# A Mamba-2 scan on one core: one gate SiLU, the first exponentials of sums and one mask product change their places

## The chip, the cores and the metric

One core of one Trainium2 chip runs the whole program. The metric is the device time in microseconds; lower is better. Before the change it is 2375.91 us, the median of 3 runs (2374.59 to 2376.46).

## What is computed

A two-layer decoder trunk on a sequence of 1024 tokens, width 1024, in float32. Layer 0 is a sliding-window attention beside a pooling mixer; layer 1 is a Mamba-2 mixer; a SwiGLU block follows each. The change lies in the Mamba-2 mixer alone. Its inner width of 2048 falls into 4 groups of 8 heads (512 channels), and each group runs through 8 chunks of 128 tokens. Cut to what matters:

```python
def ssd_chunked(x, dt, A, Bm, Cm):
    ...
    seg = a_cs[..., :, None] - a_cs[..., None, :]
    decay = jnp.exp(jnp.where(causal, seg, -jnp.inf))
    cb = jnp.einsum('bclgn,bcsgn->bcgls', Cc, Bc)
    y_diag = jnp.einsum('bcgls,bcghls,bcsghp->bclghp', cb, decay, xdt)
    ...
    h0 = jnp.zeros((b, G, hg, p, n), jnp.float32)
    _, prev = lax.scan(step, h0, ...)
    y_off = jnp.einsum('bclgn,bcghpn,bcghl->bclghp', Cc, prev, jnp.exp(a_cs))
    return (y_diag + y_off).reshape(b, s, h, p)

y = ssd_chunked(xs, dt, A, Bm, Cm) + xs * D[:, None]
y = y.reshape(b, s, SSD_INNER) * jax.nn.silu(z)
```

Then comes an RMS norm over each group and the output projection. The carried state before the first chunk is zero, so `exp(a_cs)` of chunk 0 multiplies zero.

## The kernel before

The five engines have a program each, in a fixed order written out by hand, and wait for one another through counting semaphores. Weights come through SyncE's queue, ScalarE makes the high part of each (`hi`, L898), GpSimd the low part (`lo`, L727, 128x1024), and TensorE multiplies in three float32 passes (L1383 to L1385).

`ssd_group` runs four times (three turns of a loop, then the last group written out). In a group, per chunk c of 8:

- TensorE turns and multiplies the chunk's operands for chunk c + 1 (`token_major`, L1812), then makes the chunk's states (L1841), the part from the carried state (YOFF, L1846, not in chunk 0) and the part inside the chunk (YDIAG, L1854), which waits for the masked decay matrix of all 8 heads. Behind it come pieces of the gate projection z (`z_half`, 12 matmuls each), so many per chunk as `Z_AFTER_CHUNK` says. z has 8 blocks n, each 512 tokens of one block of 128 channels; blocks 4 to 7 are the first 512 tokens of the channel blocks b = 0 to 3. Behind chunk 7 stand two pieces (24 matmuls).
- ScalarE takes the cumulated sums, which a DMA has put into `mdec`, makes `exp` of them for the rows of YOFF (`eacs`, L1307, two instructions), then eight `Relu` (L1314) and two `Exp` (L1319) for the decay matrix. Then it does what `SILU_AFTER_CHUNK` and `HI_AFTER_CHUNK` name for the chunk: SiLU of z blocks (L1296) and high parts of weights. The exponentials of chunk c (from 2 on) wait until VectorE is through with the skip term of chunk c - 2.
- VectorE multiplies the decay matrix by the masked products in two halves (L2502, called the mask product below), copies the next chunk's operands (L2476 to L2483), then makes the new state (L2514), YOFF times `eacs` (L2521), plus YDIAG (L2524), and the skip term: four instructions `scalar_tensor_tensor` of 128x128 (L2531), which add D times x and write `yx`. `gate_first_half(b)` (L2491) multiplies the first 512 tokens of `yx` by the SiLU of z. `GATE_AFTER_CHUNK` puts b = 0 and 1 into chunk 6; b = 2 and 3 come behind the scan.
- GpSimd scales `xdt` (L852) and the state (`decayed`, L855; it waits for the state of the chunk before), then makes the low parts of weights that `LO_AFTER_CHUNK` names: number 9 in chunk 1, 10 in chunk 2, 11 in chunk 6, 12 and 13 in chunk 7.

Behind the scan ScalarE squares each gated block (L1329) and makes its high part `y_hi` (L1330), GpSimd adds the squares (L865), and VectorE makes the low part (`lo`, L2541; `y_lo`). The output projection starts with three early parts (`EARLY_OUTS`) over the blocks b = 0, 1, 2, three matmuls per block. The first of them waits block by block for `y_lo`.

## Time and profile before

| | us |
|---|---|
| median of 3 runs | 2375.91 |
| the profiled execution | 2377.45 |
| its span, first to last instruction | 2375.7 |
| TensorE busy in the span | 2310.3 |
| VectorE, ScalarE, GpSimd busy | 1269.2, 1067.4, 1207.6 |
| mean granted TensorE clock | 0.992 |

A view of the profile gives the start of an instruction (or of a run of equal ones) in us from the span's start, its duration, the engine, the line of the code, what it writes and reads, how often, and in brackets the idle time of the engine before it with what ended it. The scan of the first group runs from about 1030 to 1094 us. The four groups repeat at a distance of about 189 us, and their instructions stand at the same distances within a few hundredths of a us, but for the clock of TensorE behind chunk 7.

### The profile page before, as it was taken

How to read it: one execution, taken by the hardware profiler on the slowest of the kernel's cores; microseconds unless marked ns; L12 is line 12 of the kernel's file. 1: busy time of each engine (PE TensorE's matmuls, PEld its weight loads, DVE VectorE, ACT ScalarE, POOL GpSimd, SP SyncE). 2: the span in 40 equal slices, each digit the busy share in tenths (PEclk: the TensorE clock that was granted, in tenths of full speed). 3: DMA queues.
4: the chain of work that ended last, by engine and by line, in shares of the span. 5: the costliest groups of instructions: out<-in, count | busy, mean ns of one | idle time of the engine just before them, and what ended most of it. 6: DMA issues, size and time to landing. Idle time of an engine off the chain costs nothing.

```text
span 2375.7 us, 29380 instructions
## 1 busy us (share of the span) xinstructions
PE 2310.3 (97%) x10850; PEld 1882.3 (79%) x10850; DVE 1269.2 (53%) x1662; ACT 1067.4 (45%) x1888; POOL 1207.6 (51%) x852
## 2 busy tenths in 40 slices
PE   7999999999999999999999999999999999999997
PEld 5867778888888888777877887887878888887886
DVE  6447563333336787467257347438762433335776
ACT  4036553333333446375266248238543333333444
POOL 3223287777774654224224214314287777774653
PEclk9999999999999999999999999999999999999999
DMA  5100223323238753121221212122213323227744
GB/s 154 49 27 19 102 65 118 115 85 115 85 111 287 243 151 94 56 81 54 63 71 54 67 41 89 39 59 80 91 61 132 116 84 116 85 98 275 254 148 142
DMA packets 166786, 247.89 MB, mean 104 GB/s; under 512 B 18416, under 2 KB 111484, under 8 KB 164092
## 3 DMA queue, kind: packets, MB, share of 16 engines
q1 hardware_dynamic: 161020, 230.06, 29.7%
q10 hardware_dynamic: 5632, 15.99, 1.7%
q8 instruction: 90, 1.47, 0.3%
q14 instruction: 44, 0.36, 0.0%
HBM read 192.93 MB, written 53.08 MB: 104 GB/s over the span
## 4 chain that ended last, share of the span: by engine, by line
PE 85%; DVE 6%; issue 2%; ACT 2%; POOL 2%; DMA 1%; SPq 0%; DVEq 0%; ACTq 0%; POOLq 0%
PE ps L1383 27%; PE ps L1385 26%; PE ps L1384 26%; PE ps L1854 1%; POOL p_lo L752 1%; PE ps L1406 1%; DVE acc L2463 1%; PE ps L1841 1%; DVE mdec L2502 1%; DMA d_val<-in_w_down 1%; PE ps L1548 1%; DVE yx L2531 1%; POOL p_val L776 1%; PE ps L1846 1%; PE ps L1569 1%
## 5 line engine op out<-in xcount | busy, mean ns | idle before, releaser
L727 POOL TENSOR_TENSOR w_lo<-w_raw,w_hi 128x1024 fp32r<-128x1024 f32 x74 | 181.2, 2453 | 337.2 <-ACT w_hi L898 327.0
L829 POOL TENSOR_TENSOR s_lo<-s_val,s_hi 128x512 fp32r<-128x512 f32 x154 | 233.8, 1520 | 207.9 <-ACT s_hi L1199 207.7
L1383 PE MATMUL ps<-xn_hi,w_hi 128*128 128x512 f32 x800 | 319.5, 399 | 5.0 <-DVE xn_lo L1976 2.5
L2134 DVE TENSOR_TENSOR xres<-ps,xres 128x512 f32<-128x512 f32 x132 | 90.8, 689 | 433.6 <-PE ps L1385 422.5
L1384 PE MATMUL ps<-xn_lo,w_hi 128*128 128x512 f32 x800 | 314.1, 393 | 0.0
L1385 PE MATMUL ps<-xn_hi,w_lo 128*128 128x512 f32 x800 | 313.7, 392 | 0.0
L1383 PE MATMUL ps<-xn_hi,p_hi 128*128 128x512 f32 x704 | 274.5, 390 | 0.8 <-POOL p_lo L752 0.6
L1385 PE MATMUL ps<-xn_hi,p_lo 128*128 128x512 f32 x704 | 273.9, 389 | 0.0
L1384 PE MATMUL ps<-xn_lo,p_hi 128*128 128x512 f32 x704 | 273.9, 389 | 0.0
L752 POOL TENSOR_TENSOR p_lo<-p_val,p_hi 128x512 fp32r<-128x512 f32 x176 | 237.3, 1357 | 36.5 <-ACT p_hi L1018 36.5
L1018 ACT ACTIVATE p_hi<-p_val 128x512 fp32r<-128x512 f32 x176 | 111.2, 632 | 306.8 <-POOL p_val L776 306.8
L1383 PE MATMUL ps<-d_hi,s_hi 128*128 128x512 f32 x616 | 240.5, 390 | 2.9 <-DVE d_lo L2186 2.9
L1385 PE MATMUL ps<-d_hi,s_lo 128*128 128x512 f32 x616 | 239.8, 389 | 0.0
L1384 PE MATMUL ps<-d_lo,s_hi 128*128 128x512 f32 x616 | 239.6, 389 | 0.0
L1383 PEld LDWEIGHTS ps<-xn_hi,w_hi 128*128 128x128 f32 x800 | 151.8, 190 | 43.2 <-issue 10.0
L2463 DVE SCALAR_TENSOR_TENSOR acc<-ps,gc,acc 128x1023 f32<-128x1023 f32 (+2 forms) x72 | 92.3, 1282 | 171.7 <-ACT acc L1279 170.0
L1199 ACT ACTIVATE s_hi<-s_val 128x512 fp32r<-128x512 f32 x154 | 97.1, 631 | 183.6 <-DMA d_val<-in_w_down 99.9
L1385 PEld LDWEIGHTS ps<-xn_hi,w_lo 128*128 128x128 f32 x800 | 151.7, 190 | 32.5
L1384 PEld LDWEIGHTS ps<-xn_lo,w_hi 128*128 128x128 f32 x800 | 152.0, 190 | 30.2
L898 ACT ACTIVATE w_hi<-w_raw 128x1024 fp32r<-128x1024 f32 x72 | 75.1, 1052 | 206.2 <-PE ps L1385 181.7
L1383 PEld LDWEIGHTS ps<-xn_hi,p_hi 128*128 128x128 f32 x704 | 132.2, 188 | 28.4 <-POOL p_lo L752 1.2
L852 POOL TENSOR_TENSOR xds<-xdt,gc 128x512 f32<-128x512 f32 x32 | 33.5, 1047 | 237.2 <-DVE xdt L2483 237.2
(269 smaller groups left out, 5160.0 us busy)
## 6 DMA issues: line engine op xcount, KB each, us to landing
s_val<-hidden SPq DMA_DIRECT2D x154, 256.0 KB, 2.8
hidden<-xres SPq DMA_DIRECT2D x20, 1792.0 KB, 6.6
wv_g<-in_w_gate SPq DMA_DIRECT2D x22, 1024.0 KB, 5.3
wv_u<-in_w_up SPq DMA_DIRECT2D x22, 1024.0 KB, 5.2
w_raw<-in_ssd_w_in SPq DMA_DIRECT2D x40, 512.0 KB, 3.9
d_val<-in_w_down SPq DMA_DIRECT2D x70, 256.0 KB, 4.0
rows_v<-in_w_down SPq DMA_DIRECT2D x64, 256.0 KB, 3.6
mdec<-decay_sums SPq DMA_DIRECT2D x32, 512.0 KB, 3.7
```

Source lines behind the costliest of these rows:

```text
L727: pool.tensor_tensor(w_lo[piece.slot][:, :], raw[piece.raw][:, :], f(w_hi[piece.slot][:, :]), ALU.subtract).then_inc(lo_done, 1)
L752: pool.tensor_tensor(p_lo[n][:, :, :], src, f(p_hi[n][:, :, :]), ALU.subtract).then_inc(p_lo_done, 1)
L829: pool.tensor_tensor(s_lo[i][:, :], s_val[i][:, :], f(s_hi[i][:, :]), ALU.subtract)\
L852: pool.tensor_tensor(heads(xds), heads(xdt[c % 2]), factor(GC_DS), ALU.mult).then_inc(xds_ready, 1)
L898: act.activation(w_hi[piece.slot][:, :], raw[piece.raw][:, :], ACT.Copy).then_inc(hi_done, 1)
L1018: act.activation(p_hi[n][:, :, :], src, ACT.Copy).then_inc(p_hi_done, 1)
L1199: act.activation(s_hi[i][:, :], s_val[i][:, :], ACT.Copy).then_inc(s_hi_done, 1)
L1383: pe.matmul(dst, l_hi, r_hi, start=first, stop=False, skip_group_check=reopened)
L1384: pe.matmul(dst, l_hi, r_lo, start=False, stop=False, skip_group_check=reopened)
L1385: return pe.matmul(dst, l_lo, r_hi, start=False, stop=last, skip_group_check=reopened)
L2134: dve.tensor_tensor(tmp, bank, tmp, ALU.add).then_inc(c_ready, 1)
L2463: ins = dve.scalar_tensor_tensor(acc[k % 2][:, shift:], full[:, 0:S - shift], gc[:, tap:tap + 1], acc[k % 2][:, shift:], ALU.mult, ALU.add)
```

## The change

Five edits, all in `ssd_group` and its tables.

1. The SiLU of z block 5 (channel block 1, first 512 tokens) moves on ScalarE from behind chunk 5's exponentials to behind chunk 7's. VectorE's product with it, `gate_first_half(1)`, moves from chunk 6 to behind the scan, ahead of `gate_first_half(2)`. ScalarE waits at the end of chunk 6 until TensorE has made z block 5, since the next high part overwrites its weights.
2. The two `eacs` exponentials of chunk 0, which nothing reads, are left out.
3. In chunk 6 VectorE makes the mask product of chunk 7 right behind the YDIAG addition and ahead of the skip term of chunk 6. Until now it stood behind that skip term.
4. TensorE's YDIAG of a chunk waits until YDIAG of the chunk before has been read (`ydiag_read`), no longer until its skip term is done. YOFF of chunk 1 waits for no reading any more.
5. VectorE's addition of YDIAG signals `ydiag_read` in place of the step counter.

```diff
-        SILU_AFTER_CHUNK = {1: (0, 1), 3: (2, 3), 5: (4, 5), 7: (6,)}
-        GATE_AFTER_CHUNK = {6: (0, 1)}
+        SILU_AFTER_CHUNK = {1: (0, 1), 3: (2, 3), 5: (4,), 7: (5, 6)}
+        GATE_AFTER_CHUNK = {6: (0,)}
...
-                    if c >= 2:
-                        act.wait_ge(y_ready, t.count("chunk", c - 1))
-                    for odd in range(2):
-                        rows = slice(64 * odd, 64 * odd + 64)
-                        ins = act.activation(eacs[c % 2][rows, :, :], m[rows, odd::2, :], ACT.Exp)
-                    ins.then_inc(e_ready, 1)
-                    act.wait_ge(e_ready, t.count("chunk", c + 1))
-
+                    if c:
+                        if c >= 2:
+                            act.wait_ge(y_ready, t.count("chunk", c - 1))
+                        for odd in range(2):
+                            rows = slice(64 * odd, 64 * odd + 64)
+                            ins = act.activation(eacs[c % 2][rows, :, :], m[rows, odd::2, :], ACT.Exp)
+                        ins.then_inc(e_ready, 1)
+                        act.wait_ge(e_ready, t.count("carry", c))
...
+                    if c == NT - 2:
+                        act.wait_ge(z_full, t.count("z", 6))
...
                     if c:
-                        pe.wait_ge(yoff_read, t.count("chunk", c))
+                        if c >= 2:
+                            pe.wait_ge(yoff_read, t.count("carry", c - 1))
...
                     if c:
-                        pe.wait_ge(y_ready, t.count("chunk", c))
+                        pe.wait_ge(ydiag_read, t.count("chunk", c))
...
+                    if c < NT - 1:
+                        masked_decay(c)
...
-                        step(dve.tensor_tensor(e2, ps[:, YDIAG, :], e2, ALU.add))
+                        dve.tensor_tensor(e2, ps[:, YDIAG, :], e2, ALU.add).then_inc(ydiag_read, 1)
                     else:
                         dve.wait_ge(ydiag_full, t.count("chunk", c + 1))
-                        dve.tensor_copy(e2, ps[:, YDIAG, :]).then_inc(yoff_read, 1)
-                        dve.wait_ge(yoff_read, t.count("chunk", c + 1))
+                        dve.tensor_copy(e2, ps[:, YDIAG, :]).then_inc(ydiag_read, 1)
+                    if c == NT - 2:
+                        masked_decay(c + 1)
+                    dve.wait_ge(ydiag_read, t.count("chunk", c + 1))
                     for b in range(BG):
...
+                gate_first_half(1)
                 gate_first_half(2)
```

`masked_decay(c)` is the old pair of mask products of chunk c, unchanged.

## Rows read from the trace of the kernel before

**Rows 1.** The page's busy times of the engines, with share and instructions.
```profile
PE 2310.3 (97%) x10850; PEld 1882.3 (79%) x10850; DVE 1269.2 (53%) x1662; ACT 1067.4 (45%) x1888; POOL 1207.6 (51%) x852
```
**Rows 2.** Waits of TensorE, whole span: us in total, times, longest.
```profile
PE ps L1854 <- DVE mdec L2502: 14.6, 13, 2.6
```
**Rows 3.** Timeline of TensorE, first group, chunks 1 and 7.
```profile
1043.28 1.09 PE L1854 MATMUL ps<-mdec,xdt 128*64 128x128 f32 x16 [0.82 <-DVE mdec L2502]
...
1092.53 1.09 PE L1854 MATMUL ps<-mdec,xdt 128*64 128x128 f32 x16 [2.56 <-DVE mdec L2502]
```
**Rows 4.** Stretches behind chunk 7, groups 1, 2 and 4: busy, clock, DMA.
```profile
1090.00:1105.00 15.00, 12.47 (x59) 0.89 0.26 72
1279.00:1294.00 15.00, 12.46 (x56) 0.77 0.26 70
...
1659.00:1674.00 15.00, 12.41 (x68) 1.00 0.22 72
```
**Rows 5.** Timeline of VectorE, first group: chunks 0, 5 and 6, behind the scan.
```profile
1038.06 3.96 DVE L2531 SCALAR_TENSOR_TENSOR yx<-yx,gc,eacs 128x128 f32<-128x128 f32 x4
...
1079.61 3.30 DVE L2531 SCALAR_TENSOR_TENSOR yx<-yx,gc,eacs 128x128 f32<-128x128 f32 x4
...
1085.03 1.28 DVE L2491 TENSOR_TENSOR yx<-ps,yx 128x512 f32<-128x512 f32 x2
1086.22 0.68 DVE L2514 TENSOR_TENSOR state<-ps,decayed 128x512 f32<-128x512 f32 x1
...
1087.54 0.69 DVE L2524 TENSOR_TENSOR eacs<-ps,eacs 128x512 f32<-128x512 f32 x1
1088.26 3.01 DVE L2531 SCALAR_TENSOR_TENSOR yx<-yx,gc,eacs 128x128 f32<-128x128 f32 x4
1091.20 1.28 DVE L2502 TENSOR_TENSOR mdec<-mdec,cbm 128x512 f32<-128x512 f32 x2
...
1096.18 3.54 DVE L2541 SCALAR_TENSOR_TENSOR y_lo<-yx,gc,y_hi 128x512 fp32r<-128x512 f32 x3
```
**Rows 6.** Timeline of GpSimd in the same stretches.
```profile
1038.92 2.43 POOL L727 TENSOR_TENSOR w_lo<-w_raw,w_hi 128x1024 fp32r<-128x1024 f32 x1
...
1086.98 1.05 POOL L855 TENSOR_TENSOR decayed<-state,gc 128x512 f32<-128x512 f32 x1 [0.75 <-DVE state L2514]
1087.99 2.35 POOL L727 TENSOR_TENSOR w_lo<-w_raw,w_hi 128x1024 fp32r<-128x1024 f32 x1
1091.47 3.25 POOL L727 TENSOR_TENSOR w_lo<-w_raw,w_hi 128x1024 fp32r<-128x1024 f32 x1 [1.13 <-ACT w_hi L898]
...
1097.08 1.43 POOL L865 TENSOR_TENSOR sq<-sq,sq 128x512 f32<-128x512 f32 x1 [0.27 <-ACT sq L1329]
```
**Rows 7.** Timeline of ScalarE, first group: chunk 0, chunk 7, behind the scan.
```profile
1030.08 1.27 ACT L1307 ACTIVATE eacs<-mdec 64x512 f32<-64x512 f32 x2
...
1083.62 1.25 ACT L1307 ACTIVATE eacs<-mdec 64x512 f32<-64x512 f32 x2
...
1087.39 1.15 ACT L1319 ACTIVATE mdec<-mdec 128x512 f32<-128x512 f32 x2
...
1090.34 1.05 ACT L898 ACTIVATE w_hi<-w_raw 128x1024 fp32r<-128x1024 f32 x1
...
1096.29 0.63 ACT L1329 ACTIVATE sq<-yx 128x512 f32<-128x512 f32 x1 [0.23 <-DVE yx L2491]
```
**Rows 8.** Timeline, feed-forward stage: two back-to-back VectorE products and GpSimd.
```profile
883.55 0.69 DVE L2178 TENSOR_TENSOR d_val<-rows_v,d_val 128x512 f32<-128x512 f32 x1
...
883.92 1.47 POOL L829 TENSOR_TENSOR s_lo<-s_val,s_hi 128x512 fp32r<-128x512 f32 x1 [0.92 <-ACT s_hi L1199]
...
884.15 1.79 DVE L2186 TENSOR_TENSOR d_lo<-d_val,d_hi 128x512 fp32r<-128x512 f32 x1
```
**Rows 9.** Timeline of TensorE, group 4: chunk 7's YDIAG, first early output part.
```profile
1661.90 1.09 PE L1854 MATMUL ps<-mdec,xdt 128*64 128x128 f32 x16 [2.58 <-DVE mdec L2502]
...
1668.51 0.39 PE L1383 MATMUL ps<-w_hi,y_hi 128*128 128x512 f32 x1
```

More of the change, by code:

```diff
@@ L509, in trunk @@
         states_full, yoff_full, ydiag_full = sem("states_full"), sem("yoff_full"), sem("ydiag_full")
-        yoff_read, y_ready = sem("yoff_read"), sem("y_ready")
+        yoff_read, ydiag_read, y_ready = sem("yoff_read"), sem("ydiag_read"), sem("y_ready")
         sums_full, z_full, z_gated = sem("sums_full"), sem("z_full"), sem("z_gated")
@@ L888, in _ @@
                 act.dma_start(xres[:, tt, :], x[0, tt * P:(tt + 1) * P, :]).then_inc(x_loaded[tt], 16)
-            t = Tally(unit=0, out=0, tile=0, chunk=0, loaded=0, conv=0, z=0, tail=0, group=0, ssq=0, xhi=0)
+            t = Tally(unit=0, out=0, tile=0, chunk=0, carry=0, loaded=0, conv=0, z=0, tail=0, group=0, ssq=0, xhi=0)
             def hi(piece, free=None, count=None):
@@ L1324, in ssd_group @@
                 t.add("chunk", NT)
+                t.add("carry", NT - 1)
                 t.add("loaded", 16 * NT // 2)
@@ L1361, in _ @@
             with act.Fori(0, G - 1) as g:
-                t.enter(g, unit=NCB, conv=NCB, z=2 * BG, chunk=NT, loaded=16 * NT // 2, out=2 * NT, group=1,
+                t.enter(g, unit=NCB, conv=NCB, z=2 * BG, chunk=NT, carry=NT - 1, loaded=16 * NT // 2, out=2 * NT, group=1,
                         ssq=2)
@@ L2491, in gate_first_half, with masked_decay @@
                     dve.tensor_tensor(yx[:, b, 0:BANK], ps[:, Z_BANKS[(BG + b) % 3], :], yx[:, b, 0:BANK], ALU.mult).then_inc(z_gated, 1)
-                token_major(0)
-                for c in range(NT):
-                    tok = slice(c * P, (c + 1) * P)
+                def masked_decay(c):
                     for hf in range(2):
@@ L2503, in ssd_group @@
                             .then_inc(m_ready, 1)
+                token_major(0)
+                for c in range(NT):
+                    tok = slice(c * P, (c + 1) * P)
+                    if c < NT - 1:
+                        masked_decay(c)
                     if c + 1 < NT:
@@ L2516, in ssd_group @@
                         dve.tensor_copy(state[:, :], ps[:, STATES, :]).then_inc(state_ready, 1)
-                    dve.wait_ge(e_ready, t.count("chunk", c + 1))
                     e = eacs[c % 2]
@@ L2520, in ssd_group @@
                     if c:
+                        dve.wait_ge(e_ready, t.count("carry", c))
                         dve.tensor_tensor(e2, ps[:, YOFF, :], e2, ALU.mult).then_inc(yoff_read, 1)
-                        dve.wait_ge(yoff_read, t.count("chunk", c + 1))
+                        dve.wait_ge(yoff_read, t.count("carry", c))
                         dve.wait_ge(ydiag_full, t.count("chunk", c + 1))
-                        step(dve.tensor_tensor(e2, ps[:, YDIAG, :], e2, ALU.add))
+                        dve.tensor_tensor(e2, ps[:, YDIAG, :], e2, ALU.add).then_inc(ydiag_read, 1)
                     else:
                         dve.wait_ge(ydiag_full, t.count("chunk", c + 1))
-                        dve.tensor_copy(e2, ps[:, YDIAG, :]).then_inc(yoff_read, 1)
-                        dve.wait_ge(yoff_read, t.count("chunk", c + 1))
+                        dve.tensor_copy(e2, ps[:, YDIAG, :]).then_inc(ydiag_read, 1)
+                    if c == NT - 2:
+                        masked_decay(c + 1)
+                    dve.wait_ge(ydiag_read, t.count("chunk", c + 1))
                     for b in range(BG):
@@ L2586, in _ @@
             with dve.Fori(0, G - 1) as g:
-                t.enter(g, step=(CONV - 2) * NCB + NT - 1, **dve_loop)
+                t.enter(g, step=(CONV - 2) * NCB, **dve_loop)
                 ssd_group(g)
```

## The prediction

> **What bounds the kernel now.** I read the page first: TensorE is busy 97% of the span [rows 1], so only its idle time and its slow clock can be won. Next I read its waits. In the scan one wait stands out: YDIAG (L1854) waits 14.6 us for the mask product, 13 times, at most 2.6 us [rows 2]. The timeline shows where: in each group 0.82 us ahead of chunk 1 and 2.56 us ahead of chunk 7 [rows 3]; four times these are 13.5, and the other 1.1 us are short waits ahead of chunk 6, which the change doesn't touch. Last I read the clock. The stretch behind chunk 7's wait has a mean granted clock of 0.89, 0.77, 0.89 and 1.00 in groups 1 to 4 (group 3's row is as group 1's), so it was at the level of 1.2 GHz for a part of it in three groups [rows 4]. Before each fall TensorE had been idle 2.56 us. In 15 us a mean of 0.89 costs (1 - 0.89) x 15 = 1.65 us; together 1.65 + 3.45 + 1.65 + 0 = 6.75 us. Some of this fell on gaps; I take 6.3.
>
> **Why chunk 7 waits.** VectorE's line in chunk 6 is: two gate products (1.28 us), state at 1086.22, YDIAG addition at 1087.54, skip term 1088.26 to 1091.27, mask product of chunk 7 from 1091.20 [rows 5]. The four skip instructions take 3.01 us, 2.08 of them up to 1090.34, where GpSimd's low part of weight 12 ends [rows 6]; the other 0.93 us are three of them and the end of the first, so a free one comes every 0.26 to 0.3 us and four take 1.1. The same is seen in chunk 0 (3.96 us for four, beside the low part from 1038.92) and in chunk 5 (3.30 us) [rows 5, 6]. So VectorE instructions with both operands in SBUF and GpSimd's shut each other out. That a `tensor_tensor`, such as the mask product, is shut out as well is shown by the feed-forward row: GpSimd starts at 883.92, the product of 884.15 takes 1.79 us, the one before it 0.69 [rows 8].
>
> **The change, part by part** (times of group 1).
>
> *First exponentials left out.* ScalarE gains 1.27 us in chunk 0 [rows 7], so the mask product of chunk 0 and YDIAG come up to 0.25 us earlier. But chunk 1's mask product stands behind the skip term that the low part of weight 9 holds, until 1041.3 whatever ScalarE does [rows 5, 6]; that low part follows VectorE's xdt, state and GpSimd's scaling, which come 0.1 us earlier. Gain 0.1 us per group, 0.4 in all; bounds 0 and 4 x 0.25 = 1.0.
>
> *SiLU and gate of block 5 moved.* VectorE loses one gate product from chunk 6, 0.60 us (two take 1.28, one 0.68): state at 1085.63. GpSimd's scaling starts 0.76 behind the state [rows 5, 6], so at 1086.39, and the low part of weight 12 runs 1087.39 to 1089.74. ScalarE in chunk 5 loses the wait for z block 5, but chunk 7's exponentials wait for the skip term of chunk 5, which ends at 1082.9 (1079.61 + 3.30) [rows 5]; they start 0.65 us earlier at best (was 1083.62) and end near 1087.9: the first of the two that the mask product waits for started at 1087.39, and both take 1.15 us [rows 7]. That is soon enough for the mask product. The number of table loads stays (one ahead of each run of SiLUs).
>
> *Mask product ahead of the skip term.* The YDIAG addition starts 0.60 us earlier, at 1086.94; 0.60 later (one product's pitch), at 1087.54, the mask product could start. The low part of weight 12 has started 0.15 us before it, back to back with the scaling, and holds the port. So the first half ends 0.55 us behind 1089.74, at 1090.3, the second at 1090.9. YDIAG of chunk 7 starts at 1090.94 instead of 1092.53: TensorE's wait shrinks by 1.6 us to 0.96 and doesn't vanish. If the mask product were not held, it would end at 1088.8, ahead of TensorE's arrival at 1089.97 (1092.53 - 2.56), and the wait would go.
>
> *What is late next.* Behind YDIAG stand 24 z matmuls, 5.5 us (1661.90 + 1.09 to 1668.51 [rows 9]), so TensorE comes to the early output parts at 1097.5; their third block, six matmuls on, would start at 1098.9. It needs `y_lo` of block 2, and that chain now has one gate more and starts behind the skip term. ScalarE's high part of weight 13 ended at 1091.39 [rows 7]; it moves 0.65 earlier and one SiLU (0.49) later, so GpSimd's low part of weight 13 asks for the port at 1091.29 (was 1091.47) [rows 6]. By then the skip term of chunk 6 runs: its four instructions start at 1090.8, 1091.07, 1091.33, 1091.6. In the trace this same low part asked at 1091.47, in the middle of a back-to-back run of VectorE, and waited through the next product, which started 0.33 us after it asked: 3.25 us instead of 2.4 [rows 6]. I take this as the nearest row (same instruction, same kind of run, 4 groups of 4), so the skip term is not cut. Low part 13 then runs 1091.8 to 1094.2. VectorE: state, YOFF, YDIAG addition to 1093.9; skip term, held to 1094.2, ends 1095.1; gate 1 to 1095.8, gate 2 to 1096.4. ScalarE needs about 1.2 us per block (a square takes 0.63 [rows 7], its high part as long), so `y_hi` of block 2 is there at 1098.3. The low parts fight with GpSimd's additions of squares as they do now (3.54 us for three of them, 1.43 us for an addition) [rows 5, 6]: block 1 ends at 1098.6, the second addition runs to 1099.6, block 2 ends at 1100.15. TensorE starts its third block at 1100.2, having stood 1.3 us. Today in group 4, where the clock doesn't fall, it starts 1.36 us behind 1668.51 [rows 9], at 1100.50 in group 1's times (YDIAG of chunk 7 at 1661.90 and 1092.53 [rows 3, 9]). So the gain without the clock is 0.3 us a group, 1.2 us in all; what the moved mask product wins, the moved gate gives back for the most part. Bounds: 0, and 1.6 + 1.5 per group less what group 4's own slack hides, some 1.6 us a group or 6.4.
>
> *The clock.* The longest idle stretch falls from 2.56 to 0.96 us, with 0.3 and 0.9 more some 8 us later. The nearest row is the 0.82 us of chunk 1 [rows 3], behind which the clock stayed at 1.00 in all four groups. So I take it that the falls go: 6.3 us. Bounds 0 and 6.75.
>
> *The rest.* The weaker waits of TensorE (edit 4) gain nothing: the mask product of the same chunk comes after the skip term in all chunks but the last, and there it is the one counted. ScalarE's new wait for z block 5 in chunk 6 is met: its last piece stands behind chunk 4 on TensorE, two chunks ahead; if it weren't, high part 12 and the exponentials of chunk 7 would queue behind it. No DMA is moved past another; SyncE's load of weight 13 waits for low part 11, which stays where it is.
>
> **Sum.** 0.4 + 1.2 + 6.3 = 7.9 us. The profiled execution took 2377.45 with a span of 2375.7, 1.5 us above the median; its like would have a span of 2367.8. From the median: 2375.9 - 7.9 = **2368.0 us**. A run of this kernel can be told from no change at about 0.2%, 4.75 us.
>
> **The rivals.**
>
> *The low part of weight 13 cuts into the skip term (slower).* It asks 0.31 us before the fourth skip instruction starts; in the feed-forward row GpSimd asked 0.23 us before the second product and won [rows 8]. Then the skip term of chunk 6 ends at 1094.1 instead of 1091.9, the YDIAG addition at 1096.1, gate 1 at 1097.8, gate 2 at 1098.4, `y_lo` of block 2 at 1102.1. TensorE starts the third block at 1102.15, 1.65 us later than today's 1100.50, and stands 1.6, 0.8 and 0.9 us between single blocks, 3.3 us in 4.6, so the clock falls as it does now. Four times 1.65 less 0.4 is 6.2 us slower: 2382.1 us. It decides if GpSimd gets the port before 1091.6. If the clock held all the same, it would end at 2375.8. The rows speak both ways, hence 0.27.
>
> The Trainium skill (SBUF — State Buffer, section "Who interferes with whom") says of these two engines that whoever issues first gets the shared pair for the whole instruction. By it GpSimd, asking at 1091.29, would come ahead of the last skip instruction, and this rival's time would follow; the trace agrees at 883.92 and disagrees at 1091.47, where GpSimd came first and the second product still went ahead [rows 6, 8].
>
> *The clock falls all the same (no change).* With 0.96 and 1.25 us of idling within 10 us it may. Then 0.4 + 1.2 = 1.6 us: 2374.3 us. For it: nobody has seen this kernel stand for between 0.82 and 2.56 us. Chance 0.15.
>
> *The low part of block 2 goes ahead of the second addition of squares (faster).* Then TensorE's third block starts at 1099.3; 0.9 us more a group, and with a free port all three blocks lie hidden: up to 12.5 us, 2363.4 us. Against it: today's addition at 1097.08 won against a low part that stood ready [rows 5, 6]. Chance 0.08.
>
> **How the numbers follow.** Forecast 0.50, its own range 2365 to 2371. Faster by over 0.2%: 0.49 of it and 0.07 of the last rival, 0.56. Slower: 0.17 of the first rival, its other 0.10 being within 0.2%. Same: 0.10 + 0.15 + 0.02 = 0.27. The range reaches from the last rival, 2363, into the first, 2381; outside lie 0.03 below and 0.13 above.
>
> **What would show it.** Right: chunk 7's YDIAG waits about 1.0 us, the mask product's first half takes some 2.7 us beside low part 12, low part 13 takes about 2.9 us and the four skip instructions of chunk 6 only 1.1; a new wait of L1383 for `y_lo` of about 1 us a group; mean clock 1.00 in all four stretches. Wrong: skip instructions of chunk 6 of over 3 us (first rival), clocks of 0.77 to 0.89 (second), no wait for `y_lo` (third). The prediction fails as a whole if the exponentials of chunk 7 end later than 1087.9.

## The result, and the profile after

The changed kernel takes 2384.46 us (median of 6 runs, 2382.01 to 2386.73); the kernel before, on the same chip in the same rounds, 2375.25 us. The ratio is 1.004, with a 95% interval of 1.0027 to 1.0053: slower by 0.4%, 9.2 us, where I had forecast 2368.0 us, and outside my range, which ended at 2381. The profiled execution took 2386.73 us with a span of 2385.0.

The page's line of busy times, against [rows 1], and the waits of TensorE (us in total, times, longest), against [rows 2]:

```profile
PE 2312.2 (97%) x10850; PEld 1880.0 (79%) x10850; DVE 1284.0 (54%) x1662; ACT 1062.2 (45%) x1880; POOL 1208.0 (51%) x852
```
```profile
PE ps L1386 <- DVE y_lo L2551: 11.7, 12, 1.5
PE ps L1858 <- DVE mdec L2504: 8.3, 12, 1.0
```

Of the counted instructions only ScalarE's eight exponentials are gone, yet VectorE is busy 14.8 us longer: some of its instructions last longer. The wait for the mask product (now L2504) fell from 14.6 to 8.3 us, and a wait that the kernel before had nowhere, of the output matmuls (L1386) for `y_lo` (L2551), came to 11.7 us, three in each group. TensorE's timeline shows both (start, duration; in brackets the idle time and its releaser; against [rows 3, 9]); the first two rows are chunk 0 of groups 1 and 2:

```profile
1038.72 1.09 PE L1858 MATMUL ps<-mdec,xdt 128*64 128x128 f32 x16
...
1228.58 1.09 PE L1858 MATMUL ps<-mdec,xdt 128*64 128x128 f32 x16
```
```profile
1093.84 1.09 PE L1858 MATMUL ps<-mdec,xdt 128*64 128x128 f32 x16 [1.01 <-DVE mdec L2504]
...
1102.14 0.47 PE L1386 MATMUL ps<-w_hi,y_hi 128*128 128x512 f32 x1 [1.54 <-DVE y_lo L2551]
...
1103.84 0.47 PE L1386 MATMUL ps<-w_hi,y_hi 128*128 128x512 f32 x1 [0.76 <-DVE y_lo L2551]
...
1105.53 0.47 PE L1386 MATMUL ps<-w_hi,y_hi 128*128 128x512 f32 x1 [0.75 <-DVE y_lo L2551]
```

Chunk 7's YDIAG waits 1.01 us instead of 2.56: 1.5 us won in each group. But the third block of the early output part starts 11.69 us behind it (1105.53 - 1093.84), where it started 7.96 us behind it before ([rows 9]: 1668.51 and two pitches of 0.68, against 1661.90). From chunk 0 to chunk 7 the scan takes 55.12 us (before 56.65), so the third block comes 66.8 us behind chunk 0's YDIAG instead of 64.6: 2.2 us late, and four times 2.2 is 8.8 us of the 9.2.

Why it is late stands in VectorE's line (against [rows 5]):

```profile
1082.50 3.29 DVE L2541 SCALAR_TENSOR_TENSOR yx<-yx,gc,eacs 128x128 f32<-128x128 f32 x4
...
1087.91 0.67 DVE L2495 TENSOR_TENSOR yx<-ps,yx 128x512 f32<-128x512 f32 x1
1088.51 0.67 DVE L2522 TENSOR_TENSOR state<-ps,decayed 128x512 f32<-128x512 f32 x1
...
1090.42 3.36 DVE L2504 TENSOR_TENSOR mdec<-mdec,cbm 128x512 f32<-128x512 f32 x2
1093.71 3.33 DVE L2541 SCALAR_TENSOR_TENSOR yx<-yx,gc,eacs 128x128 f32<-128x128 f32 x4
...
1098.99 1.14 DVE L2541 SCALAR_TENSOR_TENSOR yx<-yx,gc,eacs 128x128 f32<-128x128 f32 x4
1100.05 1.28 DVE L2495 TENSOR_TENSOR yx<-ps,yx 128x512 f32<-128x512 f32 x2
1101.25 4.13 DVE L2551 SCALAR_TENSOR_TENSOR y_lo<-yx,gc,y_hi 128x512 fp32r<-128x512 f32 x3
```

and in GpSimd's (against [rows 6]):

```profile
1090.27 2.37 POOL L727 TENSOR_TENSOR w_lo<-w_raw,w_hi 128x1024 fp32r<-128x1024 f32 x1
1094.23 2.39 POOL L727 TENSOR_TENSOR w_lo<-w_raw,w_hi 128x1024 fp32r<-128x1024 f32 x1 [1.60 <-ACT w_hi L898]
1101.47 3.35 POOL L865 TENSOR_TENSOR sq<-sq,sq 128x512 f32<-128x512 f32 x2 [4.85 <-ACT sq L1332]
```

The mask product (1090.42) is held by the low part of weight 12, as forecast: 3.36 us for two. The skip term of chunk 6 (1093.71) takes 3.33 us for four instructions, where the free one behind it (1098.99) takes 1.14. The low part of weight 13 starts at 1094.23 and lasts 2.39 us, so it was not held; in the kernel before it waited and took 3.25. It cut into the skip term, and everything behind it on VectorE moved: state, YOFF, YDIAG addition, skip term 7, gates 1 and 2, and the first `y_lo`, which starts at 1101.25, 7.41 us behind YDIAG. The stretch from 1094.2 us on shows which skip instruction of the first group lost; the line covers the second and the third of the four:

```profile
1093.97 2.80 DVE L2541 SCALAR_TENSOR_TENSOR yx<-yx,gc,eacs 128x128 f32<-128x128 f32 x2
```

This pair is the second instruction, still running, and the third, started at 1094.234 in the trace, one nanosecond behind GpSimd's 1094.233: it took 2.54 us. Some skip instruction loses in all four groups of this execution and of a second one (after_again below), but not always the same. The third loses in four of these eight groups; in the other four the third still takes its 0.34 us, the low part waits for it, and the fourth loses. Group 4 of this execution is such a case: its third instruction started 4 ns ahead of GpSimd, and these are GpSimd's line and the fourth instruction:

```profile
1667.48 2.59 POOL L727 TENSOR_TENSOR w_lo<-w_raw,w_hi 128x1024 fp32r<-128x1024 f32 x1 [1.60 <-ACT w_hi L898]
```
```profile
1667.74 2.48 DVE L2541 SCALAR_TENSOR_TENSOR yx<-yx,gc,eacs 128x128 f32<-128x128 f32 x1
```

The loss is the same in both cases: the third block starts 11.61 to 11.69 us behind YDIAG in all eight groups.

ScalarE (against [rows 7]) does what was forecast; the chunk-7 exponentials end in time and the high part of weight 13 ends at 1094.16. One square and one `y_hi` later it waits 4.54 us for gate 1:

```profile
1085.88 1.27 ACT L1308 ACTIVATE eacs<-mdec 64x512 f32<-64x512 f32 x2 [4.19 <-DVE yx L2541]
...
1089.66 1.15 ACT L1319 ACTIVATE mdec<-mdec 128x512 f32<-128x512 f32 x2
...
1093.10 1.06 ACT L898 ACTIVATE w_hi<-w_raw 128x1024 fp32r<-128x1024 f32 x1
...
1100.77 0.63 ACT L1332 ACTIVATE sq<-yx 128x512 f32<-128x512 f32 x1 [4.54 <-DVE yx L2495]
```

The clock (stretches: PE, PEld, DVE, ACT, POOL busy, granted clock, DMA; against [rows 4]). Right behind chunk 7's YDIAG, where the kernel before had its falls, it now stays at the level of 2.4 GHz in all groups. It falls to 1.2 GHz in groups 2 and 3 later, 10.4 and 10.6 us behind that YDIAG, when the first two of the three waits for `y_lo` are over and the third is still to come:

```profile
1090.00:1105.00 15.00, 11.46 (x61) 8.24 (x59) 14.88 (x19) 8.23 (x13) 8.30 (x5) 1.00 0.25 70
...
1293.00:1308.00 15.00, 13.87 (x58) 11.05 (x59) 11.19 (x13) 8.77 (x15) 5.83 (x6) 0.89 0.01 1
...
1484.00:1499.00 15.00, 13.76 (x51) 10.85 (x52) 9.50 (x12) 7.36 (x12) 4.29 (x4) 0.77 0.00 1
```

### The profile page after: what moved, and what is told of

It reads as the page before. It is cut to its first block, busy times and chain, and to the rows that moved or that the text cites. A ratio compares the mean times of both kernels' runs of the same rounds, so it can differ in the third digit from the quotient of the medians.

```text
span 2385.0 us, 29383 instructions
## 1 busy us (share of the span) xinstructions
PE 2312.2 (97%) x10850; PEld 1880.0 (79%) x10850; DVE 1284.0 (54%) x1662; ACT 1062.2 (45%) x1880; POOL 1208.0 (51%) x852
## 4 chain that ended last, share of the span: by engine, by line
PE 85%; DVE 7%; issue 3%; POOL 2%; ACT 1%; DMA 1%; SPq 0%; DVEq 0%; ACTq 0%; POOLq 0%
PE ps L1386 27%; PE ps L1388 26%; PE ps L1387 26%; POOL p_lo L752 1%; DVE yx L2541 1%; PE ps L1858 1%; PE ps L1844 1%; PE ps L1409 1%; DMA d_val<-in_w_down 1%; POOL p_val L776 1%; PE ps L1551 1%; PE ps L1572 1%; PE ps L1850 1%; DVE mdec L2504 1%; DVE y_lo L2551 1%
## 5 line engine op out<-in xcount | busy, mean ns | idle before, releaser
L1386 PE MATMUL ps<-xn_hi,w_hi 128*128 128x512 f32 x800 | 318.1, 398 | 5.0 <-DVE xn_lo L1980 2.5
L1386 PE MATMUL ps<-xn_hi,p_hi 128*128 128x512 f32 x704 | 274.5, 390 | 0.1
L1386 PE MATMUL ps<-d_hi,s_hi 128*128 128x512 f32 x616 | 240.5, 390 | 3.9 <-DVE d_lo L2190 3.9
L1386 PEld LDWEIGHTS ps<-xn_hi,w_hi 128*128 128x128 f32 x800 | 150.9, 189 | 42.5 <-issue 9.7
L1388 PEld LDWEIGHTS ps<-xn_hi,p_lo 128*128 128x128 f32 x704 | 132.1, 188 | 27.7
L1386 PEld LDWEIGHTS ps<-xn_hi,p_hi 128*128 128x128 f32 x704 | 132.1, 188 | 27.7 <-POOL p_lo L752 0.6
```

The source lines that it names most:

```text
L1386: pe.matmul(dst, l_hi, r_hi, start=first, stop=False, skip_group_check=reopened)
L1388: return pe.matmul(dst, l_lo, r_hi, start=False, stop=last, skip_group_check=reopened)
```

## A measure for the experiments

From the first YDIAG of one group to that of the next is a period. Where the clock doesn't fall in between, it repeats within 0.4 us in one kernel, while the part of the program ahead of the first scan varies by up to 4.5 us from one execution to the next and blurs the whole time. After: 1228.58 - 1038.72 = 189.9 us, its only period without a fall in two executions. Before: 187.6, from before_again and from before_early13, whose scan waits as that of the kernel before. The difference, 2.3 us, times four is 9 us and explains the measured 9.2 us; that the two agree so well is partly luck, since the interval of the latter reaches from 6.4 to 12.6 us and the falls of the clock are in it.

Each row compares a kernel with the kernel before in the same rounds. The last four columns are us from the profiled execution; the first three of them agree within 0.12 us between the groups of one kernel (apart_mask_first's third block: 9.13 to 9.59), and the third block and the period are those of groups without a fall.

| kernel | median, us (runs) | before beside it | ratio (95%) | YDIAG wait, chunk 7 | chunk 0 to 7 | third block behind YDIAG 7 | period |
|---|---|---|---|---|---|---|---|
| before | 2375.25 (6) | | | 2.56 | 56.65 | 7.96 | 187.6 |
| after | 2384.46 (6) | 2375.25 | 1.004 (1.0027 to 1.0053) | 1.01 | 55.12 | 11.68 | 189.9 |
| hold13 | 2372.30 (10) | 2373.36 | 0.9996 (0.9986 to 1.0006) | 1.01 | 55.13 | 9.90 | 188.0 |
| hold12_13 | 2376.71 (10) | 2373.36 | 1.0009 (0.9997 to 1.0021) | none | 54.08 | 11.03 | 188.1 |
| gate_back | 2374.66 (10) | 2373.36 | 1.0007 (0.9995 to 1.0019) | 1.58 | 55.72 | 9.99 | 188.7 |
| gate_only | 2373.41 (10) | 2373.36 | 0.9993 (0.9981 to 1.0004) | 1.99 | 56.09 | 8.54 | 188.0 |
| apart_skip_first | 2356.43 (4) | 2373.56 | 0.993 (0.9913 to 0.9947) | none | 52.82 | 8.20 | 184.1 |
| apart_mask_first | 2361.89 (4) | 2373.56 | 0.9955 (0.9939 to 0.9972) | none | 52.82 | 9.45 | 185.3 |
| before_apart | 2361.97 (5) | 2372.0 | 0.9955 (0.9941 to 0.9969) | 0.70 | 53.88 | 8.25 | 185.4 |
| apart_exps_back | 2357.14 (4) | 2372.0 | 0.9936 (0.992 to 0.9953) | none | 52.82 | 8.20 | 184.2 |

## The experiments

**hold13: the cut taken away from the changed kernel.** GpSimd waits until skip term 6 is done before it starts the low part of weight 13.

```
                     for k in LO_AFTER_CHUNK.get(c, ()):
+                        if k == 13:
+                            pool.wait_ge(y_ready, t.count("chunk", NT - 1))
                         lo(piece(k))
```

> The changed kernel with one wait more: GpSimd starts the low part of weight 13 only when the skip term of chunk 6 is done. Theory A (the cut): in the changed kernel this low part takes the port in front of the third of the four skip instructions of chunk 6 (asked at 1094.233, the third came at 1094.234) and holds it 2.4 us; y_lo of block 2, and so TensorE's third early output block, come 2 us late. Then with this wait the four skip instructions take 1.1 us (not 3.3), TensorE's wait for y_lo falls from 2.9 to about 1.3 us a group, the third block starts about 9.3 us behind YDIAG of chunk 7 (now 11.7), and the kernel is some 10 us (4 x 2.4) faster than the changed one, more if the clock no longer falls; ratio to the kernel before 0.995 to 1.000. Rival B (the moved gate itself makes the chain late, or the loss lies elsewhere, as in the 2.8 us by which the changed kernel's first scan starts later): no more than 3 us are won, ratio 1.002 or more.

Measured: 2372.3 us, 1.1 us less than the kernel before beside it (2373.36). The changed kernel was 9.2 us slower than its own, so hold13 wins 10.3 us, as theory A had it; the third block comes 9.9 us behind YDIAG, not 9.3. VectorE, GpSimd and TensorE of hold13, first group:

```profile
1089.50 1.13 DVE L2543 SCALAR_TENSOR_TENSOR yx<-yx,gc,eacs 128x128 f32<-128x128 f32 x4
...
1092.59 1.55 DVE L2543 SCALAR_TENSOR_TENSOR yx<-yx,gc,eacs 128x128 f32<-128x128 f32 x4
1094.06 1.28 DVE L2497 TENSOR_TENSOR yx<-ps,yx 128x512 f32<-128x512 f32 x2
1095.26 4.14 DVE L2553 SCALAR_TENSOR_TENSOR y_lo<-yx,gc,y_hi 128x512 fp32r<-128x512 f32 x3
```
```profile
1090.79 2.41 POOL L727 TENSOR_TENSOR w_lo<-w_raw,w_hi 128x1024 fp32r<-128x1024 f32 x1 [2.36 <-DVE yx L2543]
```
```profile
1089.63 1.09 PE L1860 MATMUL ps<-mdec,xdt 128*64 128x128 f32 x16 [1.01 <-DVE mdec L2506]
...
1099.54 0.47 PE L1388 MATMUL ps<-w_hi,y_hi 128*128 128x512 f32 x1 [0.75 <-DVE y_lo L2553]
```

Skip term 6 takes 1.13 us again, and the period loses 1.9 of its 2.3 us. So the cut makes the loss of the changed kernel. But hold13 is also the case that I had forecast for the change (wait of 1.0, free skip term, no clock fall in the scan), and it is no faster than the kernel before: its third block comes 55.13 + 9.90 = 65.0 us behind chunk 0, against 64.6.

**hold12_13: the low part of weight 12 held as well**, until the mask product is done.

```
+                        if k == 12:
+                            pool.wait_ge(m_ready, t.count("half", 2 * NT))
```

> The changed kernel with two waits: GpSimd starts the low part of weight 12 only behind the mask product of chunk 7, and that of weight 13 only behind the skip term of chunk 6. Theory A: the mask product's first half takes 0.68 us (now 2.76), YDIAG of chunk 7 waits for nothing (now 1.0 us). But low part 12 then stands before the skip term of chunk 6 and holds it for 2.4 us, so that y_lo comes as late as with low part 13 held alone or 1 us later; the wait only moves. Ratio to the kernel before 0.995 to 1.001, at most 1 us from the first run of this set. Rival: the wait of 1.0 us at YDIAG is worth its full length: 4 us faster than the first run.

Measured: 2376.71 us. YDIAG's wait is gone, and nothing is won. The periods without a fall are as long as hold13's (188.1 and 188.0 us), but the median is 4.4 us above it, where theory A allowed 1 us; the clock fell for 6.8 us in one group of the profiled execution and in none of hold13's, which may be the difference and isn't shown. VectorE and GpSimd of hold12_13:

```profile
1089.63 1.28 DVE L2509 TENSOR_TENSOR mdec<-mdec,cbm 128x512 f32<-128x512 f32 x2
1090.83 3.28 DVE L2546 SCALAR_TENSOR_TENSOR yx<-yx,gc,eacs 128x128 f32<-128x128 f32 x4
```
```profile
1091.08 2.37 POOL L727 TENSOR_TENSOR w_lo<-w_raw,w_hi 128x1024 fp32r<-128x1024 f32 x1 [1.56 <-DVE mdec L2509]
```

The mask product is free (1.28), and the low part cuts the skip term behind it instead (3.28). The 2.4 us stay on VectorE; the waits for `y_lo`, 5.9 us in all in hold13, come to 9.4. To move one low part by one instruction moves the loss, it doesn't remove it.

**gate_back: the changed kernel with the SiLU and gate of block 5 where they were.**

```
-        SILU_AFTER_CHUNK = {1: (0, 1), 3: (2, 3), 5: (4,), 7: (5, 6)}
-        GATE_AFTER_CHUNK = {6: (0,)}
+        SILU_AFTER_CHUNK = {1: (0, 1), 3: (2, 3), 5: (4, 5), 7: (6,)}
+        GATE_AFTER_CHUNK = {6: (0, 1)}
...
-                    if c == NT - 2:
-                        act.wait_ge(z_full, t.count("z", 6))
...
-                gate_first_half(1)
                 gate_first_half(2)
```

> The changed kernel with the SiLU and the gate of block 5 back in chunks 5 and 6; the other edits stay. Theory A: state of chunk 6 and low part 12 come 0.6 us later, so the mask product is held until about 0.6 us later, YDIAG of chunk 7 waits 1.6 us. Low part 13 asks 0.5 us earlier (one SiLU less ahead of it), which is in the middle of the mask product's first half or at its end: if it wins there, the second half is held 2.4 us and YDIAG waits 4 us (ratio 1.002 to 1.006); if it loses, it comes into the skip term as now. The chain to y_lo is two blocks' gate shorter in either case. Rival B (the moved gate is the cause): YDIAG waits 1.6 us, no wait for y_lo, ratio 0.995 to 0.998.

Measured: 2374.66 us, YDIAG wait 1.58 (0.57 more than in the changed kernel: the gate's 0.60), skip term 6 cut all the same: it takes 3.25 us, with the low part asking 0.05 us behind the start of its first instruction (the expectation had it ask inside the mask product). The third block comes 55.72 + 9.99 = 65.7 us behind chunk 0, 1.1 us earlier than in the changed kernel. So it is the mask product's new place that puts the skip term in the low part's way, with the gate or without. But the cut alone isn't the whole loss: with the gate in its old place the period is 188.7 us instead of 189.9, and the kernel can't be told from the kernel before (1.0007). The two edits together make the 2.3 us a period; where low part 13 interrupts the skip term, the gate behind the scan costs `y_lo` more than it gives YDIAG.

**gate_only: the kernel before with the moved gate alone** (the same three edits the other way round, in the kernel before).

> The kernel before with nothing but the moved SiLU and gate of block 5. Theory A: the cut needs both the mask product ahead of the skip term and the moved SiLU. Here the skip term of chunk 6 is held by low part 12 as before, 0.6 us earlier, low part 13 asks in the mask product's second half and waits for it; YDIAG of chunk 7 waits 2.0 us (was 2.56), y_lo of block 2 comes 0.3 us earlier than before against the group's start. Ratio 0.998 to 1.000. Rival B (the moved gate makes the loss): ratio 1.002 to 1.004, with TensorE waiting 2 us or more a group for y_lo.

Measured: 2373.41 us against 2373.36: nothing. Low part 12 alone holds the skip term, as before. YDIAG's wait shrinks to 1.99, and the third block comes 0.6 us later behind it, so the 0.3 us expected for `y_lo` aren't there: what the gate gives in chunk 6 it takes behind the scan.

**before_again and after_again: both kernels once more**, to see what repeats.

> The kernel before once more, for its clock. The prediction took three falls of the clock behind chunk 7, 13.6 us at 1.2 GHz, from one profiled execution (2377.45 us), though that one lies above the median of all runs since (2373.4). If such falls belong to every execution, this profile has them in three or four groups again. If they are by chance, it has fewer or others, and YDIAG of chunk 7 waits 2.56 us in each group all the same.

> The changed kernel once more. The cut by low part 13 came at a distance of 1 ns between its start and that of the third skip instruction. If it is by chance, the three waits for y_lo (1.5, 0.9 and 0.9 us) are missing in some group of this execution; if it is in the order of the work, all four groups have them. Falls of the clock behind the scan in other groups than in the first profile would show that these are by chance.

Measured: 2374.48 and 2384.69 us, one run each. The 2.56 us stand in every group of the first, the cut and the 1.0 us in every group of the second. What does not repeat is the clock: the kernel before had fallen to the level of 1.2 GHz behind chunk 7 in three of four groups in the first execution (the trace gives 3.4, 6.8 and 3.4 us), and now did so in one, for 3.4 us. In the changed kernel it fell in two groups in the first execution (3.4 and 6.8 us) and in three in the second (3.4, 3.4 and 6.8 us). Of the stretches of before_again this is the one with the fall:

```profile
1092.00:1107.00 15.00, 12.42 (x61) 9.98 (x61) 12.36 (x20) 8.30 (x14) 8.11 (x5) 0.89 0.26 72
```

**before_early13: does the low part always cut if it asks first?** In the kernel before, the high part of weight 13 goes ahead of the last SiLU, so that the low part asks earlier, still ahead of the mask product.

```
                     for n in SILU_AFTER_CHUNK.get(c, ()):
+                        if n == 6:
+                            act.wait_ge(z_full, t.count("z", 7))
+                            table(ACT.Silu)
+                            hi(piece(GP - 1))
                         silu_z(n)
                     for k in HI_AFTER_CHUNK.get(c, ()):
-                        hi(piece(k))
+                        if k < GP - 1:
+                            hi(piece(k))
```

> The kernel before with the high part of weight 13 ahead of the last SiLU of chunk 7 on ScalarE (its table loaded by a small instruction first), so that GpSimd's low part 13 asks for the port 0.3 us earlier, at the start of the mask product's first half and not 0.27 us into it. In the kernel before the second half, 0.33 us behind the asking, still went ahead, in all four groups. If a run of VectorE products keeps the port, nothing changes: both halves 0.68 us, YDIAG of chunk 7 waits 2.56 us. If who asks first wins, the second half (or both) is held for 2.4 us and YDIAG of chunk 7 waits about 5 us.

Measured: 2371.64 us. VectorE (stretch from 1091.9 us), GpSimd and the stretches of groups 1 and 2:

```profile
1091.61 0.60 DVE L2536 SCALAR_TENSOR_TENSOR yx<-yx,gc,eacs 128x128 f32<-128x128 f32 x2
1092.13 1.28 DVE L2507 TENSOR_TENSOR mdec<-mdec,cbm 128x512 f32<-128x512 f32 x2
```
```profile
1092.01 3.65 POOL L727 TENSOR_TENSOR w_lo<-w_raw,w_hi 128x1024 fp32r<-128x1024 f32 x1 [0.74 <-ACT w_hi L898]
```
```profile
1090.00:1105.00 15.00, 12.46 (x71) 10.28 (x70) 13.92 (x22) 9.95 (x15) 8.94 (x5) 1.00 0.26 72
1278.00:1293.00 15.00, 12.42 (x70) 10.19 (x69) 13.97 (x22) 9.78 (x15) 8.65 (x5) 1.00 0.26 71
```

GpSimd asks at 1092.01, while the last skip instruction runs and 0.12 us ahead of the mask product, and waits through both halves of it (3.65 us instead of 2.4). It is so in all four groups. In the changed kernel it asks in the same place, while a skip instruction runs, and a skip instruction behind it loses. So the order of asking alone doesn't decide; what stands next on VectorE does too. The second finding: TensorE waited 2.54 to 2.58 us ahead of chunk 7 in all four groups, and the clock fell behind none.

**apart_skip_first and apart_mask_first: four low parts out of the way of chunks 0, 5, 6 and 7.** Low part 9 waits for the mask product of chunk 1, low part 11 comes with chunk 5, low part 12 waits for the last mask product, low part 13 goes behind the second addition of squares; gate 1 comes in chunk 7, ahead of its state. In the first the last mask product stands behind the skip term, as in the kernel before; in the second ahead of it.

```
-        LO_AFTER_CHUNK = {1: (9,), 2: (10,), 6: (11,), 7: (12, 13)}
+        LO_AFTER_CHUNK = {1: (9,), 2: (10,), 5: (11,), 7: (12,)}
-        SILU_AFTER_CHUNK = {1: (0, 1), 3: (2, 3), 5: (4,), 7: (5, 6)}
-        GATE_AFTER_CHUNK = {6: (0,)}
+        SILU_AFTER_CHUNK = {1: (0, 1), 3: (2, 3), 5: (4,), 6: (5,), 7: (6,)}
+        GATE_AFTER_CHUNK = {6: (0,), 7: (1,)}
...
+                        if k == 9:
+                            pool.wait_ge(m_ready, t.count("half", 4))
+                        if k == 12:
+                            pool.wait_ge(m_ready, t.count("half", 2 * NT))
...
+                        if (h, b) == (0, 2):
+                            lo(piece(GP - 1))
```

> A version meant to keep GpSimd's weight low parts away from VectorE's products in SBUF. From the changed kernel: the mask product of chunk 7 stands behind the skip term again; the SiLU of block 5 goes behind chunk 6's exponentials and its gate into chunk 7; low part 9 waits for the mask product of chunk 1, low part 11 moves from chunk 6 to chunk 5, low part 12 waits for the mask product of chunk 7, low part 13 comes behind the second addition of squares. Theory A (the port makes all the waits of the scan): no skip term of chunks 0, 5 and 6 over 1.4 us, YDIAG never waits more than 0.2 us (now 0.87, 0.22 and 1.0 us), the first scan takes 53.0 us from YDIAG of chunk 0 to that of chunk 7 (now 55.1), the third early output part block starts at most 8.6 us behind it, ratio to the kernel before 0.993 to 0.997. Rival (ScalarE's exponentials set chunk 7): YDIAG of chunk 7 still waits 0.5 to 1.5 us for them.

> The same with the mask product of chunk 7 ahead of the skip term of chunk 6, as in the changed kernel. Theory A: with the low parts out of the way the order is of no use, since ScalarE's exponentials of chunk 7 end behind the YDIAG addition of chunk 6: the skip term then waits for them with the mask product, and low part 12 is let go in front of the skip term and holds it. So y_lo comes up to 2 us a group later than in the version before this, ratio 0.995 to 1.000. Rival: the order helps by itself, and this one is the faster of the two.

Measured: 2356.43 us (0.993) and 2361.89 us (0.9955). The first is 17 us faster than the kernel before beside it and so some 26 us faster than the changed one (17.1 + 9.2). Its VectorE and GpSimd around chunks 5 to 7, and its TensorE at chunk 7:

```profile
1079.06 1.14 DVE L2543 SCALAR_TENSOR_TENSOR yx<-yx,gc,eacs 128x128 f32<-128x128 f32 x4
...
1085.98 1.14 DVE L2543 SCALAR_TENSOR_TENSOR yx<-yx,gc,eacs 128x128 f32<-128x128 f32 x4
1087.04 1.28 DVE L2509 TENSOR_TENSOR mdec<-mdec,cbm 128x512 f32<-128x512 f32 x2
...
1091.26 2.20 DVE L2543 SCALAR_TENSOR_TENSOR yx<-yx,gc,eacs 128x128 f32<-128x128 f32 x4
```
```profile
1088.48 2.38 POOL L727 TENSOR_TENSOR w_lo<-w_raw,w_hi 128x1024 fp32r<-128x1024 f32 x1 [2.73 <-DVE mdec L2509]
...
1096.50 2.86 POOL L727 TENSOR_TENSOR w_lo<-w_raw,w_hi 128x1024 fp32r<-128x1024 f32 x1
```
```profile
1089.04 1.09 PE L1863 MATMUL ps<-mdec,xdt 128*64 128x128 f32 x16
```

No YDIAG waits any more. The low part of weight 12 starts at 1088.48, where VectorE's line holds a gate, a state, the YOFF product and the YDIAG addition, all of which read PSUM, and they keep their 0.68 to 0.69 us. VectorE isn't free of GpSimd everywhere: the skip term of chunk 0 takes 1.84 us (the expectation allowed 1.4), and low part 10, which wasn't moved, still cuts that of chunk 2 (one instruction takes 2.48 us); neither reaches TensorE. With the mask product ahead, the same low part meets skip term 6 and cuts it (3.28 us for four), so this order costs 1.2 us a period: with the low parts in good places the reordering is a loss of 5.5 us.

**before_apart: the low parts alone, in the kernel before** (the waits of low parts 9 and 12 and the new place of 13, as above).

> The kernel before with the waits of GpSimd's low parts alone: low part 9 waits for the mask product of chunk 1, low part 12 for that of chunk 7, low part 13 comes behind the second addition of squares; low part 11, the SiLUs, the gates, the order of VectorE and the first exponentials stay. Theory A (the shared port made chunk 7's wait, not the order of VectorE's work): the four skip instructions of chunk 6 take 1.1 us (3.0 before), YDIAG of chunk 7 waits 0.7 us or less (2.56 before), chunk 1's waits for nothing; some 2.7 us a group, so the kernel is 10 to 14 us faster than before with the clock, ratio 0.994 to 0.997. Rival (the order matters, the port only moves the waits): ratio 0.998 or more.

Measured: 2361.97 us (0.9955), 10 us less than the kernel before, with nothing reordered on VectorE. The four skip instructions of chunk 6 take 1.14 us, YDIAG's wait at chunk 7 is 0.70 us, at chunk 1 none, all as theory A had it.

**apart_exps_back: the first exponentials put back** into the best version (`if c:` becomes `if True:`, with the counts that belong to it).

> The fastest version so far (low parts kept apart, mask product behind the skip term) with the first chunk's exponentials of sums put back. Theory A: they cost what they delay at YDIAG of chunk 0, 0.1 to 0.25 us a group, since nothing behind them is late now but the mask product of chunk 1: ratio within 0.001 of 0.993. Rival: with chunk 1's wait gone the 1.27 us of ScalarE come through to YDIAG of chunk 1 and cost up to 5 us in all, ratio 0.995.

Measured: 2357.14 us against 2356.43, a period 0.1 us longer. The intervals of the two overlap, and the periods of one kernel differ by more than 0.1 us, so the eight exponentials are worth at most some tenths of a us in all and can't be told from nothing. The rival's 5 us are ruled out.

## Why the prediction was wrong

**Right: chunk 7's wait and what sets it.** Forecast 0.96 us, measured 1.01; the first half of the mask product was to take 2.7 us beside low part 12 and took 2.76. ScalarE's exponentials, forecast to end by 1087.9 with YDIAG 7 at 1090.94, ended 3.0 us ahead of YDIAG as forecast. The moved SiLU added no wait for z block 5, the number of table loads stayed, and the weaker waits of TensorE gained nothing that can be seen, though no run takes them alone.

**Not contradicted: the first exponentials.** Forecast 0.1 us a group. YDIAG of chunk 0 no longer waits (before, 0.08 to 0.15 us), chunk 1 gives 0.05 back (0.87 instead of 0.82), and apart_exps_back differs by 0.1 a period, which is within the spread.

**Wrong, and it decided the sign: "I take this as the nearest row".** That step gave the skip term of chunk 6 a free way, because in the kernel before the low part of weight 13 had asked first and waited [rows 6]. But that row shows the mask product next on VectorE, and with the new order skip instructions stand next. The row with the same instructions on both sides was there: in chunk 0 the low part from 1038.92 starts 0.86 us into a skip term, takes 2.43 us, so it isn't held, and the skip term takes 3.96 [rows 5, 6]. The same stands in chunk 2: there the low part from 1046.31 starts 0.13 us ahead of a skip instruction, while another runs, and that skip instruction takes 2.49 us. I took a price from these rows and not the order. before_early13 shows the mask product winning again with an earlier ask, 0.12 us ahead; after, after_again and gate_back show skip instructions losing, in every group. The first rival had it right, and its chain follows the measured one: shifted by the 2.90 us by which YDIAG 7 comes later than in my times, the skip term ends at 1094.14 (rival: 1094.1), the YDIAG addition at 1096.06 (1096.1), gate 1 at 1097.83 (1097.8), gate 2 at 1098.43 (1098.4). My own times had the warning in them: they put the request at 1091.29 and the third skip instruction at 1091.33, so 0.04 us decided between the third and the fourth. The trace shows the two starts within 9 ns in all eight groups, and it didn't matter: where the third got through, the fourth lost, as the rival says.

**Wrong in size: the `y_lo` chain.** Rival and forecast alike gave the three `y_lo` products 3.7 us from the end of gate 2; they took 4.05 in the changed kernel and in hold13, beside two additions of squares that run back to back (3.35 us from 1101.47). With these 0.35 us, and 0.15 instead of 0.05 from their end to TensorE's start, the rival's 1.65 us a group becomes 2.1; measured 2.2. In hold13 the low part of weight 13 also cost skip term 7 0.4 us. So the forecast's gain of 0.3 us a group was in truth a loss of 0.4 us (65.0 against 64.6).

**Wrong in size: the clock, 6.3 us.** The falls did cost that in the profiled execution: the three periods with a fall exceed 187.6 us by 1.7, 3.3 and 1.6 us. But they are not a constant of the kernel. With the same waits, three executions (before, before_again, before_early13) showed 3, 1 and 0 falls in four groups. I subtracted the falls of one execution from the median of others. What an average execution loses by them can only be estimated. hold13 had no fall in its scan and is 1.1 us faster than the kernel before, though its four periods are 1.6 us longer, which leaves about 2.7 us for the clock of the kernel before; the other kernels without falls (apart_skip_first, apart_mask_first, before_apart and gate_back) give 1.2 to 3.1 us by the same comparison. These figures take one execution for all of a kernel's, and the interval of hold13's time alone is 2.4 us to either side. A second estimate uses every run: its mean granted clock c is known, and (1 - c) times its span (over the whole program) is 16.7 us in the mean of 31 runs of the kernel before and 13.0 us in that of hold13's ten, 3.7 us less; for the other four kernels it is 3.5 to 5.8 us less than for the runs of the kernel before beside them. So the falls are worth something between 1 and 6 us, and 6.3 was too much for the forecast case; how much too much stays open.

The forecast case was measured in hold13: -1.1 us instead of -7.9. In the case that came true, four periods are 9 us longer, and nothing is won on the clock, since the new waits bring falls of their own: they lengthen the periods of the changed kernel by 3.6 us in the first execution and by 4.7 us in the second, against 6.6 and 1.9 us in those of the kernel before.

**A slip in a rival's sum.** The third rival's gain of 12.5 us doesn't follow from its terms: a third block at 1099.3 instead of 1100.50 gives 4 x 1.2 + 0.4 + 6.3 = 11.5 us. Nothing hangs on it.

**The rule on the shared pair.** The trace of before had the low part waiting though it asked first, in all four groups, and before_early13 repeated it; after the change it went ahead of the skip instruction. The Trainium skill (SBUF — State Buffer, section "Who interferes with whom") says of VectorE's two-port modes that whoever issues first gets the pair for the whole instruction, and of the contest in general that the order of issue decides and not the shape of the operation. The skip instructions agree with it to within 3 ns: the third instructions that started 4 to 9 ns ahead of GpSimd (three groups) kept their 0.34 us, those behind it lost, as the fourth did at 0.26 us behind; of the three at 0 to 3 ns ahead one kept its 0.34 us and two lost. The mask products of before and before_early13 do not agree. I was right to doubt the rule and wrong about where the doubt applied.

## What to carry to other kernels

When an instruction is moved, look at what then stands next to each transfer of a shared resource: the row that tells how a contest ends is the one with the same instruction on both sides, and where the rows speak both ways, the rival deserves as much chance as the forecast. A wait that such a contest makes was removed here by moving GpSimd's long instructions, above all to where VectorE reads PSUM: three low parts moved in the kernel before gave 10 us. Reordering VectorE (the change itself) or holding a low part back behind one instruction (hold12_13) only moved the loss. A clock term taken from one execution is a sample: take it from several, or compare periods without a fall.

## What the runs showed of the hardware

- When a low part of GpSimd asks while a VectorE instruction on SBUF runs, the outcome depends on the VectorE instruction that comes next: a skip instruction (`scalar_tensor_tensor`, 128x128) loses 2.2 us, in every group of every run here, and the mask product (`tensor_tensor`, 128x512, its second operand broadcast) goes ahead of a low part that asked 0.12 or 0.33 us before it (before, before_again, before_early13) or 0.05 to 0.50 us before it (low part 11 in chunk 5 of the two apart kernels). It is not the kind of operation alone, since `d_lo`, a `tensor_tensor` too, was held [rows 8]; nor is the mask product immune, since it was held 2.1 us where low part 12 had followed the scaling back to back (1090.27, 0.15 us ahead of it) and VectorE was at an instruction that reads PSUM. What sets it apart, the broadcast, its own semaphores or something else, was not tried and stays open. Where the two starts lie within 3 ns, either of them can come first (the eight groups of after and after_again).
- Instructions of VectorE with an operand in PSUM keep their 0.67 to 0.69 us beside a low part: in apart_skip_first gate, state, YOFF product and YDIAG addition all ran between 1088.24 and 1091.23, with low part 12 beside them from 1088.48 to 1090.86.
- TensorE's clock fell to the level of 1.2 GHz after idle stretches of 2.56 us in some executions and not in others of the same kernel; in the changed kernel it fell behind the first two of the waits of about 1.5, 0.76 and 0.75 us, in two groups of four in one execution and in three of four in the other; behind hold13's 0.76 and 0.75 us alone it didn't fall.
- The part ahead of the first scan took between 1034.5 and 1039.0 us in kernels that don't differ there, so single executions can't tell less than that apart.
